# One exponential and one masked product per head and chunk in the state-space rounds of a hybrid encoder, with GpSimd weighting the inner products

## The reference, cut to what matters

```
seg = acs[:, :, :, None] - acs[:, :, None, :]
Lm = jnp.exp(jnp.where(mask, seg, -jnp.inf))
CB = jnp.einsum('bctgn,bcsgn->bctsg', Cc, Bc)
y_diag = jnp.einsum('bctsg,bctsgh,bcsghp->bctghp', CB, Lm, xdt)
```

## Time and profile before

| | |
|---|---|
| median of 3 runs | 2295.68 us (2295.66 to 2299.93) |
| profiled execution | 2296.97 us, span 2295.4 us |
| PE busy | 2243.4 us (98%) |
| DVE, ACT, POOL busy | 1457.2 (63%), 1019.1 (44%), 373.2 us (16%) |
| rounds of the four groups | about 662 to 962 us of the span |
| three loop passes | 83.5 us each: PE busy 81.8, DVE 74.0, ACT 48.9, POOL 15.6 |
| mean granted TensorE clock | 0.995 |

### The profile page before, as it was taken

How to read it: one execution, slowest core, us unless ns; L and a number is a source line. 1 busy time by engine, 2 the same in 40 slices (tenths; PEclk the granted TensorE clock), 3 DMA queues, 4 the chain that set the end, 5 groups by cost and what they waited for, 6 DMA issues and landing times.

```text
span 2295.4 us, 36398 instructions
## 1 busy us (share of the span) xinstructions
PE 2243.4 (98%) x13156; PEld 2001.7 (87%) x13156; DVE 1457.2 (63%) x2331; ACT 1019.1 (44%) x1659; POOL 373.2 (16%) x257
## 2 busy tenths in 40 slices
PE   8999999998999999999999999999999999999998
PEld 6999999997888787888888888888888899899997
DVE  7677676777879889423555555552246667677676
ACT  6333242334454754623555665644234334242345
POOL 2000000001012201133333333322333000000000
PEclk9999999999999999999999999999999999999999
DMA  3222221213211111132111111111342222231212
GB/s 121 67 74 56 66 81 55 73 37 108 68 34 32 37 46 37 47 92 83 47 47 46 46 46 46 44 31 48 104 133 67 70 75 56 61 86 55 73 38 92
DMA packets 252289, 144.65 MB, mean 63 GB/s; under 512 B 5728, under 2 KB 248592, under 8 KB 252192
## 3 DMA queue, kind: packets, MB, share of 16 engines
q1 hardware_dynamic: 249072, 130.63, 20.5%
q0 software_dynamic: 2352, 12.58, 1.6%
q10 hardware_dynamic: 768, 0.13, 0.0%
HBM read 133.89 MB, written 9.44 MB: 62 GB/s over the span
## 4 chain that ended last, share of the span: by engine, by line
PE 78%; DVE 11%; issue 5%; ACT 3%; POOL 1%; DMA 0%; ACTq 0%; DVEq 0%; POOLq 0%; SPq 0%
PE slot L525 33%; PE aux L556 22%; PE slot L605 14%; DVE ca L1983 1%; DVE wlo L1910 1%; PE aux L932 1%; PE aux L900 1%; POOL wlo L2332 1%; PE aux L824 1%; PE aux L914 1%; PE aux L811 1%; PE aux L925 1%; PE slot L693 1%; PE aux L889 1%; DVE wlo L1678 1%
## 5 line engine op out<-in xcount | busy, mean ns | idle before, releaser
L2332 POOL TENSOR_TENSOR wlo<-raw,whi 128x1024 fp32r<-128x1024 f32 (+1 forms) x100 | 232.2, 2322 | 1027.7 <-ACT whi L1021 1027.7
L525 PE MATMUL slot<-xh,whi 128*128 128x256 f32 (+1 forms) x1360 | 364.9, 350 | 10.3 <-DVE wlo L1910 3.7
L525 PE MATMUL slot<-xh,wlo 128*128 128x256 f32 (+1 forms) x1360 | 351.2, 340 | 0.0
L525 PE MATMUL slot<-xl,whi 128*128 128x256 f32 (+1 forms) x1360 | 350.1, 339 | 0.0
L525 PEld LDWEIGHTS slot<-xh,whi 128*128 128x128 f32 x1360 | 249.3, 188 | 52.6 <-issue 16.5
L525 PEld LDWEIGHTS slot<-xh,wlo 128*128 128x128 f32 x1360 | 255.6, 188 | 30.1
L525 PEld LDWEIGHTS slot<-xl,whi 128*128 128x128 f32 x1360 | 255.4, 188 | 29.8
L556 PE MATMUL aux<-th,whi 128*128 128x392 f32 (+1 forms) x640 | 221.1, 345 | 9.0 <-ACT work L1138 5.0
L1112 ACT ACTIVATE whi<-work 128x512 fp32r<-128x512 f32 x220 | 135.2, 624 | 198.6 <-DVE work L1699 105.0
L556 PE MATMUL aux<-tl,whi 128*128 128x392 f32 (+1 forms) x640 | 216.6, 338 | 0.0
L556 PE MATMUL aux<-th,wlo 128*128 128x392 f32 (+1 forms) x640 | 216.4, 338 | 0.0
(11 more groups left out here) (346 smaller groups left out, 4344.7 us busy)
## 6 DMA issues: line engine op xcount, KB each, us to landing
raw<-in_w_in SPq DMA_DIRECT2D x81, 512.0 KB, 3.9
raw<-in_ffn_w_gate_up SPq DMA_DIRECT2D x48, 512.0 KB, 4.2
work<-in_ffn_w_gate_up SPq DMA_DIRECT2D x40, 512.0 KB, 4.7
raw<-in_ffn_w_down SPq DMA_DIRECT2D x80, 256.0 KB, 3.1
raw<-in_ssd_w_proj SPq DMA_DIRECT2D x8, 512.0 KB, 4.0
raw<-in_hg_w_proj SPq DMA_DIRECT2D x8, 512.0 KB, 3.9
raw<-in_w_out SPq DMA_DIRECT2D x8, 512.0 KB, 4.0
h_spill<-h POOLq DMA_DIRECT2D x1, 3072.0 KB, 10.8
```

Source lines behind the costliest of these rows:

```text
L525: mm = pe.matmul(slot[b][:, PC + u:PC + v], w[b][:, t, :], x[:, t, u + off:v + off], start=(t == 0 and p == 0 and q == 0), stop=(t == k - ...
L2332: pool.tensor_tensor(wlo[s % 2][:, 0:k, :], raw[s % 2][:, 0:k, :], whi[s % 2][:, 0:k, :].bitcast(F32), ALU.subtract).then_inc(w_lo, 1)
```

## The change

- PE puts the segment sums of both directions of a chunk into one bank, `aux[c % 3]`: four matmuls accumulate there. Each direction's sums are 0 in the other's triangle, so one exponential holds both.
- ACT takes one exponential per chunk instead of per unit.
- POOL writes no `xdt`. It writes per unit `cbm` times `dt`, 128x512, into `mk[c % 2]` (direction 0) or `mb[c % 2]` (direction 1; it lies in the memory of `xw`). It may begin once `cbm` is written, and for a chunk c >= 2 once `masked` has finished chunk c - 2.
- DVE's `masked` adds the two, waits for its own result, waits for the exponential, and multiplies: two passes over 128x512 per chunk, where it had two.
- PE's outputs take `xbt` itself as weights: one product per head and chunk instead of two.
- ACT's copies into `xbt` (`ssd_turn`) wait for the outputs of the chunk that PE still reads there, instead of for POOL.

```diff
-            xdt=[[new(f"xdt{s}{d}", [P, 2 * P]) for d in range(2)] for s in range(2)],
+            mk=[new(f"mk{s}", [P, HPG, P]) for s in range(2)],
...
+        mb = [m_s["xw"][:, 2 * s:2 * s + 2, :].rearrange("p a (h t) -> p (a h) t", t=P) for s in range(2)]
...
                 for u in units:
-                    if u == 2:
+                    c, d = S_UNITS[u]
+                    if u == 4:
                         wait(pe, cbm_ok, 4, 4, G)
-                    c, d = S_UNITS[u]
...
-                    if u >= 3:
-                        wait(pe, exp_ok, 2 * NC, u - 2, G)
+                    if d == 0 and c >= 3:
+                        wait(pe, exp_ok, NC, c - 2, G)
                     for p, v in enumerate((m_s["rh"], m_s["rl"])):
-                        mm = pe.matmul(aux[u % 3][:, :], strict[d][:, :], v[u % 3][:, :, :], start=(p == 0), stop=(p == 1))
+                        mm = pe.matmul(aux[c % 3][:, :], strict[d][:, :], v[u % 3][:, :, :], start=(p == 0 and d == 0), stop=(p == 1 and d == 1))
...
-                            for d in range(2):
-                                mm = pe.matmul(aux[3][PD * (hh % 2):PD * (hh % 2 + 1), h:h + P], m_s["xdt"][c % 2][d][:, PD * hh:PD * (hh + 1)],
-                                               m_s["e"][(2 * c + d) % 4][:, hh, :], start=False, stop=(d == 1), skip_group_check=True)
+                            mm = pe.matmul(aux[3][PD * (hh % 2):PD * (hh % 2 + 1), h:h + P], m_s["xbt"][:, c + 2, PD * hh:PD * (hh + 1)],
+                                           m_s["e"][c % 4][:, hh, :], start=False, stop=True, skip_group_check=True)
...
                     if n >= 2:
-                        wait(act, xdt_ok, 2 * NC, 2 * (n - 1) - 2 * NC, G)
+                        wait(act, y_mm, 4, Y_STEP[n - 2] - 4, G)
...
-                    wait(act, seg_mm, 2 * NC, u + 1, G)
-                    wait(act, y_mm, 4, Y_STEP[(u - 4) // 2] if u >= 4 else 0, G)
-                    act.activation(m_s["e"][u % 4][:, :, :], aux[u % 3].rearrange("p (h t) -> p h t", h=HPG), ACT.Exp).then_inc(exp_ok, 1)
+                    c, d = S_UNITS[u]
+                    if d == 1:
+                        wait(act, seg_mm, 2 * NC, u + 1, G)
+                        wait(act, y_mm, 4, Y_STEP[c - 4] if c >= 4 else 0, G)
+                        act.activation(m_s["e"][c % 4][:, :, :], aux[c % 3].rearrange("p (h t) -> p h t", h=HPG), ACT.Exp).then_inc(exp_ok, 1)
...
-                wait(dve, cbm_ok, 4, 4, G)
                 for u in units:
                     c, d = S_UNITS[u]
-                    wait(dve, exp_ok, 2 * NC, u + 1, G)
-                    v = m_s["e"][u % 4][:, :, :]
-                    dve.tensor_tensor(v, v, cbm[:, d, c, :].unsqueeze(1).broadcast_to([P, HPG, P]), ALU.mult).then_inc(wy_ok, 1)
+                    if d == 0:
+                        continue
+                    m = m_s["mk"][c % 2][:, :, :]
+                    wait(dve, mk_ok, 2 * NC, 2 * c + 2, G)
+                    one(dve.tensor_tensor(m, m, mb[c % 2], ALU.add))
+                    wait(dve, exp_ok, NC, c + 1, G)
+                    v = m_s["e"][c % 4][:, :, :]
+                    dve.tensor_tensor(v, v, m, ALU.mult).then_inc(wy_ok, 1)
...
+                wait(pool, cbm_ok, 4, 4, G)
+                wait(pool, up_mm, len(S_UPD) // 2, len(S_UPD) // 2, G)
                 for u in S_STEPS[k][0]:
                     c, d = S_UNITS[u]
-                    wait(pool, y_mm, 4, Y_STEP[c - 2] if c >= 2 else 0, G)
-                    pool.tensor_tensor(h4(m_s["xdt"][c % 2][d][:, :]), h4(m_s["xbt"][:, c + 2, 0:2 * P]),
-                                       m_s["gdt"][:, c, d, :].unsqueeze(2).broadcast_to([P, HPG, PD]), ALU.mult).then_inc(xdt_ok, 1)
+                    wait(pool, wy_ok, NC, c - 1 if c >= 2 else 0, G)
+                    pool.tensor_tensor((m_s["mk"][c % 2][:, :, :], mb[c % 2])[d], cbm[:, d, c, :].unsqueeze(1).broadcast_to([P, HPG, P]),
+                                       m_s["gdt"][:, c, d, :].unsqueeze(2).broadcast_to([P, HPG, P]), ALU.mult).then_inc(mk_ok, 1)
```

More of the change, by code:

```diff
@@ L303, in build @@
         cb_mm, cbm_ok, wy_ok = sem("cb_mm"), sem("cbm_ok"), sem("wy_ok")
-        xdt_ok, y_mm, yz_ok, ya_ok = sem("xdt_ok"), sem("y_mm"), sem("yz_ok"), sem("ya_ok")
+        mk_ok, y_mm, yz_ok, ya_ok = sem("mk_ok"), sem("y_mm"), sem("yz_ok"), sem("ya_ok")
         pa_hi, pa_lo = sem("pa_hi"), sem("pa_lo")
@@ L747, in ssd_turn @@
                     else:
-                        wait(pe, exp_ok, 2 * NC, n - 2, G)
+                        wait(pe, exp_ok, NC, n - 2, G)
                     for q in range(3):
@@ L753, in ssd_updates @@
             def ssd_updates(G):
-                wait(pe, exp_ok, 2 * NC, 0, G)
+                wait(pe, exp_ok, NC, 0, G)
                 wait(pe, yz_ok, 2 * NC, 0, G)
@@ L802, in ssd_step @@
                 for u in units:
-                    if u == 2:
+                    c, d = S_UNITS[u]
+                    if u == 4:
                         wait(pe, cbm_ok, 4, 4, G)
-                    c, d = S_UNITS[u]
                     wait(pe, rh_ok, 2 * NC, u + 1, G)
                     wait(pe, rl_ok, 2 * NC, u + 1, G)
-                    if u >= 3:
-                        wait(pe, exp_ok, 2 * NC, u - 2, G)
+                    if d == 0 and c >= 3:
+                        wait(pe, exp_ok, NC, c - 2, G)
                     for p, v in enumerate((m_s["rh"], m_s["rl"])):
-                        mm = pe.matmul(aux[u % 3][:, :], strict[d][:, :], v[u % 3][:, :, :], start=(p == 0), stop=(p == 1))
+                        mm = pe.matmul(aux[c % 3][:, :], strict[d][:, :], v[u % 3][:, :, :], start=(p == 0 and d == 0), stop=(p == 1 and d == 1))
                     mm.then_inc(seg_mm, 1)
                 for c in outs:
-                    wait(pe, wy_ok, 2 * NC, 2 * c + 2, G)
-                    wait(pe, xdt_ok, 2 * NC, 2 * c + 2, G)
+                    wait(pe, wy_ok, NC, c + 1, G)
                     wait(pe, yz_ok, 2 * NC, 2 * outs[0], G)
@@ L1991, in scan_vectors @@
                 wait(dve, xw_ok, U, 0, G)
-                wait(dve, xdt_ok, 2 * NC, 0, G)
+                wait(dve, mk_ok, 2 * NC, 0, G)
                 for dst, src in (("gd", drow), ("gdt", dt_t[:, 0:NC]), ("gcd", cd_t), ("gec", ec_t),
@@ L2095, in _ @@
                 G, N = (0, g), (1, g)
-                own.enter(g, 3 + 4 * (TAPS - 1) + 2 + 7 + 6 + 4 + 3)
+                own.enter(g, 3 + 4 * (TAPS - 1) + 2 + 7 + 6 + 4 + 3 + NC)
                 conv_vectors(N)
@@ L2389, in ssd_weighted @@
                 wait(pool, up_mm, len(S_UPD) // 2, 0, G)
+                wait(pool, wy_ok, NC, 0, G)
                 for n, (d, c) in enumerate(S_UPD):
```

## The result

| | before | after |
|---|---|---|
| median, us | 2296.81 (6 runs, 2295.28 to 2299.93) | 2315.03 (6 runs, 2310.82 to 2316.29) |
| ratio | | 1.0077 (95% interval 1.0066 to 1.0088) |
| profiled execution, us | 2296.97, span 2295.4 | 2310.82, span 2309.3 |

The change makes the kernel 18 us slower. The profiled execution is the shortest of its six: its span is 13.9 us longer than that of before. The other five lie between 2314.1 and 2316.3.

What follows compares the result with a forecast made beforehand. PE and DVE, both nearly full and coupled twice a step, were taken as the bound, DVE setting the pace in a pass's second half. Three passes +16.2, fourth group -2.5, about +14 us: 2311 profiled, 2310 median; range 2292 to 2322.

Steps and rivals of the forecast that it cites:

- the walk: One loop pass followed step by step, as lateness against the times before; 5.4 us late at its end.
- gates of step 1: Up to PE's outputs in step 1: third `rh` 4.9 late, less 1.2 in hand and 0.6 of outputs, 3.1 us late.
- gates of step 2: Step 2: masks +0.9, two product pairs +4.0, less slack and 1.2 of outputs; +3.4, 6.5 us late.
- gates of step 3: Step 3: convolution -0.7, masks -0.5, chunk 5's pair +2.0, outputs -0.6; +0.2, 6.7 us late.
- end of the pass: After the last products: masks +0.4, low part 1.7 us shorter without three `xdt` ahead; 5.4 us late.
- fourth group: Last group, without convolution on DVE: first two steps cost about 1.1 us, outputs give back 3.6; -2.5 us.
- The price of a product: DVE's loss per POOL product: 1.0 us beside back-to-back products, 0.85 beside the convolution; about zero effect at 0.6.
- PE's products: One output product per direction and head goes on PE: 0.149 us each, 3.6 a group, 14.3 us in all.
- PE busy down by 14 us: Expected sign: PE's busy time over the whole span falls by 14 us.
- The cheap case: Rival: POOL steps back, a product costs DVE only 0.2 us, kernel faster at 2286 us; chance 0.15.
- POOL holding DVE through whole runs: Rival: job 1's low part waits for four products, each costs 1.17 us; 2318 us; chance 0.12.
- The clock: Rival: PE's idle before outputs of steps 1 and 2 halves the clock, +5 to +12, 2315 to 2322 us; chance 0.13.

Runs made afterwards that it cites:

- last kernel: Changed kernel with direction 0's products on ScalarE, direction 1's as VectorE multiply-adds, none on GpSimd, and ScalarE's queue reordered: 2292.37 us, ratio 0.9974.
- rearranged kernel: Changed kernel with VectorE's low part for job 5 moved ahead of `scan_vectors`, before GpSimd's run of products starts: 2314.12 us, ratio 1.0066.

## Why the prediction was right, and where it was off

The forecast was 2310 us; measured are 2315.0, and the profiled execution has 2310.8. The mechanism is the one named, and the walk holds step by step. The changed kernel's rounds begin 1.29 us later (663.56 against 662.27), a shift that stands there already in stretches that the change doesn't touch; it is taken off below. So of the 13.9 us by which the profiled spans differ, the rounds account for 12.7, and that the forecast's 14 meets the profiled time so closely owes 1.3 us to this shift, which is luck.

| lateness, us | predicted | measured |
|---|---|---|
| gates of step 1 | 3.1 | 679.85 - 675.56 - 1.29 = 3.0 |
| gates of step 2 | 6.5 | 696.31 - 688.90 - 1.29 = 6.1 |
| gates of step 3 | 6.7 | 708.96 - 701.41 - 1.29 = 6.3 |
| end of the pass | 5.4 | 88.05 - 83.45 = 4.6 |
| three passes | 16.2 | (928.80 - 663.56) - (912.21 - 662.27) = 15.3 |
| fourth group | -2.5 | 928.80 - 912.21 = 16.59 at its start, 986.95 - 973.00 = 13.95 behind it: -2.6 |

**The price of a product** was the term that decided. Predicted: 1.0 us beside back-to-back products, 0.85 beside the convolution, from an estimated 1.17 us alone less 0.15. Measured: 0.79 to 0.85 and about 0.7, from 1.04 alone. The rule "duration less 0.15", read off, is close to the 0.2 that the new rows show; the duration was interpolated between 256 and 1024 elements and came out too long. Over twelve products that is some 2 us too much a pass, and the next term takes about half of it back.

**PE's products.** Predicted 0.149 us each, 14.3 us in all, by dividing a row of eight instructions. The last kernel's trace has two heads' outputs with one product each:

```profile
674.15 0.44 PE L823 MATMUL aux<-e,xbt 128*64 128x128 f32 x4
674.52 0.33 PE L821 MATMUL aux<-ident,prev 128*128 128x128 f32 x1
```

They take 0.37 us (674.15 to 674.52) where they took 0.59, so the two removed are 0.11 us each. The pass whose products only write has PE busy for 79.19 us against 81.76: 2.6 us a group and not 3.6, about 10 us in all. The first product of such a run costs more than the later ones, and a mean of the run overrates what goes.

**PE busy down by 14 us** was expected as a sign, and it did not come: 2244.7 us against 2243.4. Without disturbance 10 us go. What fills it up fits the rows: outputs at half clock are booked with 0.70 us for 0.44, and segment sums behind a wait with 0.50 for 0.39; they were not added up. Busy time of PE was a bad sign to choose.

**The rivals.** The cheap case (0.2 us a product, break-even at 0.6) fell with the `rh` rows at 1.19 and 1.47 us each; the write-only kernel shows a case near it, 2287 us against the 2286 worked out, though with products that cost next to nothing and not 0.2 us. POOL holding DVE through whole runs did not come in the rounds: DVE's low part at 663.56 waited for one product, got its turn, and the next product waited for it. For one instruction against one, the rule of the Trainium skill (SBUF — State Buffer, Who interferes with whom), by which one excludes the other for its whole duration, is close: 0.85 of 1.04 us. At the end of the pass the run did hold DVE (5.79 us at 718.61), which costs nothing there. **The clock** is the part I undervalued. I gave it 0.13 as a case of its own, and it is instead a part of the forecast case. It fell once in each pass in the profiled execution; only the second pass is visibly longer for it, by 1.5 us. In the execution of the rearranged kernel it fell at step 2's outputs in all three, which last 4.07, 4.07 and 3.73 us for 2.45, and the three passes together are 5.1 us longer. That is about the size of the 4 us by which the usual run lies above the profiled one. The five other runs of the change have mean clocks of 0.988 to 0.990 against 0.991, but no trace of their own, so for them this is argued, not shown.

**The hidden costs** held: ACT's fewer exponentials and its new wait moved nothing, and the shorter low part gives back 33.00 against 35.15 us to the next pass, 2.15 where 1.7 was forecast. One expectation was off without effect: in the fourth group DVE waits 1.93 us for the first pair of products, where I had said under 1.

## What to carry to other kernels

A GpSimd with time to spare is not a free engine: work that reads SBUF beside VectorE's two-input products costs VectorE most of its duration, here 0.72 to 0.85 us a product, where VectorE makes the product itself in 0.61. Before moving work there, look for a row in the old trace in which the two meet, take duration less overlap as the price, and ask whether VectorE is on the path at that moment; ScalarE took half of the work at no such cost, once its own queue was put in the right order. Where PE and another engine wait for each other in turns, a run of short waits can also cost the clock, so leave some of the forecast on that side.

## What the runs showed of the hardware

- GpSimd fills of 128x512 (0.52 us) beside VectorE's two-input products cost these nothing: 1.91 us for three `rh` against 1.89. But one VectorE instruction with a single input, the first tap of the convolution, took 1.51 us beside fills and 0.63 without; why this one is held was not tested.
- A GpSimd product of only 16 elements took 0.22 us where it waited for nobody and up to 1.22 beside VectorE: what counts for it is the instruction it has to wait for.
- Turns are not always taken. Beside single products VectorE got in after one; at the end of a pass one VectorE instruction waited for nearly a whole run: for most of ten products (5.79 us), or for the rest of a run of eight (5.11 us for an instruction of 0.42). What decides between the two is open; no run was made for it.
- The granted clock fell from 2.4 to about 1.2 GHz after pauses of PE of only 0.7 us each: two in step 1 of the change's first pass came before the fall (679.01), while three in its step 2 (0.54, 0.71, 0.79) were followed by outputs at full speed. Whether this is what spreads the runs is not shown: the change's lie within 5.5 us and the last kernel's, whose trace keeps the clock in the rounds, within 3.5, but those of the kernel before, whose trace keeps it too, within 4.7.
